# A hybrid two-block transformer kernel: single instructions of ScalarE, VectorE, TensorE and the weight plan put in another order

## The chip, the cores and the metric

The kernel runs on one core of one Trainium2 chip. The metric is the device time in microseconds (us). In the notes below PE is TensorE (matrix products), ACT is ScalarE, DVE is VectorE, POOL is GpSimd and SP is SyncE, whose queue issues the loads of the weights.

## The reference, cut to what matters

256 tokens of width 1024, float32. Two blocks follow each other, of two layers each. In the first block a layer is a mixer of three branches (a chunked state-space scan, "ssd"; a latent attention of four heads, "MLA"; a spatial gate, "gMLP") and a feed-forward stage: dense in layer 0, eight experts with two chosen for each token in layer 1. In the second block the mixer has two attentions (moba, eight heads; diff, four pairs of heads) and the feed-forward stage is dense. Each half of a layer is modulated by a shift, a scale and a gate, which are products of one condition vector with large matrices.

```python
def modulation(c, w, b):
    m = jnp.einsum("bd,de->be", jax.nn.silu(c), w) + b
    shift, scale, gate = jnp.split(m, 3, axis=-1)
...
def hybrid_mixer(h, ...):
    proj = jnp.einsum("btd,de->bte", h, w_in)
    z, xs, bm, cm, dt, q_lat, kv_lat, k_pe, gu, gv = jnp.split(proj, split_at, axis=-1)
    xbc = jax.nn.silu(causal_depthwise_conv(jnp.concatenate([xs, bm, cm], axis=-1), conv_w, conv_b))
    ...
    y_ssd = gated_group_rmsnorm(ssd_scan(xs, bm, cm, dt, a_log, d_skip), z, ssd_norm_w)
    ...
    y = jnp.concatenate([y_ssd, y_mla, y_gm], axis=-1)
    return jnp.einsum("bte,ed->btd", y, w_out)

def swiglu(h, w1, w3, w2):
    a = jnp.einsum("btd,df->btf", h, w1)
    g = jnp.einsum("btd,df->btf", h, w3)
    return jnp.einsum("btf,fd->btd", jax.nn.silu(a) * g, w2)
```

## The kernel before

All weights are read in blocks of 1 MB (128 x 2048 float32), in the order of one list, `plan`, through a ring of six buffers that SP loads. A product keeps float32 accuracy by three matmuls: each operand is split into a rounded high half and the rest, its low half. ACT writes a block's high half (`high_halves`, L1261), DVE its low half in place (`low_halves`, L1956), and PE multiplies (`product`, L497 to L499):

```python
pe.matmul(ps, xh, wh, start=first, stop=False)
pe.matmul(ps, xh, wl, start=False, stop=False)
return pe.matmul(ps, xl, wh, start=False, stop=last)
```

Activations are split in the same way (`hh` and `hl`, `yl`, and `uh`/`ul`, some of which lie in buffers named `PTr`). `ahead` lets the halves run two blocks ahead of the products. Blocks of modulation matrices ("mod") stand in the plan between the others, put there by `weave`; DVE multiplies them with the condition (two instructions each, L1896) when `low_halves` comes to them, before the next low half.

Each engine's program is written out by hand as calls in order (`tensor_program`, `scalar_program`, `vector_program`, `gpsimd_program`, `sync_program`), and an engine does its instructions strictly in that order; semaphores carry the waits between engines. So an instruction that waits holds up whatever stands behind it in its engine's program. The stages follow each other: mixer, feed-forward stage, mixer, experts, mixer, feed-forward, mixer, feed-forward.

The places that the change touches are these. In the first mixer (`mixer1`): on ACT the causal convolution's Silu (`feature_gates`, L1431), behind the taps that DVE sums (L2200); the latents of MLA (L1450); the transposed queries and keys of MLA, which PE leaves in four PSUM banks and which are copied out by `heads_turned`, the second of each pair by ACT (L1469), the first by DVE (L2230), before the scores (L724). On PE, the transposes of the mixer's rows (`to_features`, L579), with eviction by ACT and the low half `yl` by DVE (L2033), and the output blocks 2 and 3, done whole in float32 (`whole_block`, L886), before blocks 0 and 1. On DVE, `gates` (the layer norm of the spatial gate) and `chunk_outputs` (which frees the bank that PE's `within_chunk`, L848, waits for). In `swiglu`: six groups of up to two blocks; `result_block` makes the halves of the block of the second matrix. `layer_rows` (L1990, L1992) applies the previous layer norm's gain and bias to the residual X before a `boundary`. In the second mixer (`mixer2`): twelve projection blocks in the order WIN2, four output blocks; `project` evicts a projection on ACT (L1589) and makes halves ahead; `next(diff)` and `next(moba)` advance the two attentions by a step, DVE evicting turned keys and queries (L2470) and ACT others.

## Time and profile before

| | |
|---|---|
| three runs, us | 2141.05 (median), 2140.62, 2142.23 |
| profiled execution | 2143.6 us |
| its span, first to last instruction | 2141.8 us, 1.8 less |
| mean granted clock of PE | 0.950 |
| busy: PE, DVE, ACT, POOL | 93%, 78%, 55%, 3% |
| DMA, mean over the span | 259 GB/s |

The stages of the span, from and to in us: start 0 to 42, first mixer layer 0 to 191, first ffn 196 to 420, first mixer layer 1 421 to 557, experts to 1394, second mixer layer 0 1410 to 1582, second ffn layer 0 1585 to 1783, second mixer layer 1 1786 to 1946, second ffn layer 1 1948 to 2141.

A profile row gives an instruction's engine, its line, what it writes and reads (`out<-in`), its shape and its time; the releaser of a wait ("<-") is the instruction whose end let the waiting one start. PEclk is the granted clock of PE as a share of full speed.

### The profile page before, as it was taken

To read this page: it belongs to the slowest core of one execution; us is meant where nothing else is said; L and a number is where in the kernel's file an instruction comes from. 1 tells how busy PE (TensorE), PEld (TensorE's weight loads), DVE (VectorE), ACT (ScalarE), POOL (GpSimd) and SP (SyncE) were. 2 spreads that over 40 slices of the span, in tenths; PEclk is the share of its full clock that TensorE was granted. 3 is DMA by queue.
4 is the path that set the end of the run, shared out by engine and by line. 5 is a ranking of instruction groups with operands and counts; after the bars stand their busy time and mean duration, and the time that the engine had idled before them with its cause. 6 is when DMAs were issued, how large, how long until landed. Compare 5 with 4: busy or idle time off the path is not lost.

```text
span 2141.8 us, 28331 instructions
## 1 busy us (share of the span) xinstructions
PE 1985.2 (93%) x11530; PEld 1716.7 (80%) x11530; DVE 1676.3 (78%) x1757; ACT 1169.2 (55%) x1312; POOL 72.7 (3%) x121
## 2 busy tenths in 40 slices
PE   6988999889789999999999999967899999889999
PEld 6776898777578888888788788766789998769998
DVE  6866888776698989899899988888778896855444
ACT  3643334364367767777777767544553445555332
POOL 6001000000100000000000000000010000000000
PEclk8988999898899999999999999988889999989999
DMA  9843899642399999999999999926229995314552
GB/s 352 282 155 138 324 350 352 232 151 93 134 339 328 348 370 354 336 354 374 337 346 358 371 331 354 335 103 229 99 99 352 348 370 169 119 59 141 192 179 99
DMA packets 251209, 554.37 MB, mean 259 GB/s; under 512 B 10076, under 2 KB 75856, under 8 KB 251072
## 3 DMA queue, kind: packets, MB, share of 16 engines
q1 hardware_dynamic: 247252, 544.13, 71.2%
q0 software_dynamic: 3552, 8.29, 1.2%
q8 instruction: 94, 1.54, 0.3%
q14 instruction: 43, 0.35, 0.0%
q10 hardware_dynamic: 268, 0.07, 0.0%
HBM read 551.40 MB, written 1.05 MB: 258 GB/s over the span
## 4 chain that ended last, share of the span: by engine, by line
PE 70%; DVE 14%; ACT 7%; DMA 5%; issue 4%; SPq 0%; ACTq 0%; DVEq 0%
PE bank L497 21%; PE bank L498 20%; PE bank L499 20%; DVE ring_lo L1956 4%; ACT ring_hi L1261 4%; DMA ring<-in_ffn_w_dram 2%; DVE acc L1896 1%; PE bank L886 1%; DMA ring<-in_w_in_dram 1%; DMA ring<-in_ada_w_dram 1%; PE bank L579 1%; PE bank L1086 1%; DVE XN L2200 1%; PE bank L548 1%; DVE work L2138 1%
## 5 line engine op out<-in xcount | busy, mean ns | idle before, releaser
L1956 DVE TENSOR_TENSOR ring_lo<-ring,ring_hi 128x2048 fp32r<-128x2048 f32 x417 | 950.0, 2286 | 270.5 <-ACT ring_hi L1261 267.8
L1261 ACT ACTIVATE ring_hi<-ring 128x2048 fp32r<-128x2048 f32 x417 | 795.5, 1913 | 487.9 <-PE bank L499 237.6
L497 PE MATMUL bank<-hh,ring_hi 128*128 128x256 f32 x1152 | 331.4, 288 | 15.0 <-DVE ring_lo L1956 9.7
L498 PE MATMUL bank<-hl,ring_hi 128*128 128x256 f32 x1152 | 329.2, 286 | 0.0
L499 PE MATMUL bank<-hh,ring_lo 128*128 128x256 f32 x1152 | 328.9, 285 | 0.0
L497 PEld LDWEIGHTS bank<-hh,ring_hi 128*128 128x128 f32 x1152 | 224.2, 195 | 18.9 <-DVE ring_lo L1956 8.6
L499 PE MATMUL bank<-ring_hi,hl 128*128 128x256 f32 (+2 forms) x768 | 238.7, 311 | 0.0
L497 PE MATMUL bank<-ring_hi,hh 128*128 128x256 f32 (+2 forms) x672 | 215.5, 321 | 14.8 <-DVE hl L2020 9.5
L497 PE MATMUL bank<-ring_hi,hgh 128*128 128x512 f32 (+1 forms) x576 | 220.3, 383 | 9.1 <-DVE ring_lo L1956 3.6
L498 PEld LDWEIGHTS bank<-hl,ring_hi 128*128 128x128 f32 x1152 | 224.3, 195 | 0.9 <-issue 0.5
L499 PEld LDWEIGHTS bank<-hh,ring_lo 128*128 128x128 f32 x1152 | 224.4, 195 | 0.0
L499 PE MATMUL bank<-ring_hi,hgl 128*128 128x512 f32 (+1 forms) x576 | 216.3, 376 | 0.0
L498 PE MATMUL bank<-ring_lo,hgh 128*128 128x512 f32 (+1 forms) x576 | 216.2, 375 | 0.0
L498 PE MATMUL bank<-ring_lo,hh 128*128 128x256 f32 (+2 forms) x672 | 209.4, 312 | 0.0
L497 PE MATMUL bank<-ring_hi,uh 128*128 128x512 f32 x496 | 198.7, 401 | 7.0 <-DVE ring_lo L1956 5.9
L498 PE MATMUL bank<-ring_lo,uh 128*128 128x512 f32 x496 | 196.2, 396 | 0.0
L499 PE MATMUL bank<-ring_hi,ul 128*128 128x512 f32 x496 | 196.0, 395 | 0.0
L1896 DVE SCALAR_TENSOR_TENSOR acc<-ring,csil,acc 128x1024 f32<-128x1024 f32 x140 | 179.7, 1283 | 14.2 <-DMA ring<-in_ada_w_dram 7.7
L497 PEld LDWEIGHTS bank<-ring_hi,hh 128*128 128x128 f32 x672 | 136.4, 203 | 30.0 <-issue 17.9
L499 PEld LDWEIGHTS bank<-ring_hi,hl 128*128 128x128 f32 x768 | 151.4, 197 | 6.6
L498 PEld LDWEIGHTS bank<-ring_lo,hh 128*128 128x128 f32 x672 | 136.5, 203 | 5.0 <-issue 0.7
L497 PEld LDWEIGHTS bank<-ring_hi,hgh 128*128 128x128 f32 x576 | 108.2, 188 | 33.9 <-issue 4.9
(426 smaller groups left out, 2795.0 us busy)
## 6 DMA issues: line engine op xcount, KB each, us to landing
ring<-in_moe_w_dram SPq DMA_DIRECT2D x264, 1024.0 KB, 5.3
ring<-in_ada_w_dram SPq DMA_DIRECT2D x48, 1024.0 KB, 8.1
ring<-in_w_mod_dram SPq DMA_DIRECT2D x48, 1024.0 KB, 7.3
ring<-in_w_in_dram SPq DMA_DIRECT2D x40, 1024.0 KB, 6.2
ring<-in_ffn_w_dram SPq DMA_DIRECT2D x33, 1024.0 KB, 6.6
ring<-in_w_gate_dram SPq DMA_DIRECT2D x22, 1024.0 KB, 5.0
ring<-in_w_up_dram SPq DMA_DIRECT2D x22, 1024.0 KB, 5.1
ring<-in_w_down_dram SPq DMA_DIRECT2D x22, 1024.0 KB, 5.1
```

The costliest lines, as they stand in the source:

```text
L497: pe.matmul(ps, xh, wh, start=first, stop=False)
L498: pe.matmul(ps, xh, wl, start=False, stop=False)
L499: return pe.matmul(ps, xl, wh, start=False, stop=last)
L548: x = pe.matmul(ps[:, 8 * j + i:8 * j + i + 1], sums_at(m, j)[0][:, 128 * i:128 * i + 128], ones[:, 0:1], start=True, stop=True)
L579: x = pe.transpose(ban[kk][:, 256 * i + 128 * t:256 * i + 128 * t + 128], src[:, t, 128 * kc:128 * kc + 128], ident)
L886: x = pe.matmul(Y[t][h][:, :], YT[:, 2 * i + k, 128 * t:128 * t + 128], w[:, c:c + 512], start=first and k == 0, stop=False)
L1086: x = pe.transpose(ps[:, 128 * c:128 * c + 128], U[:, 128 * c:128 * c + 128], ident)
L1261: act.activation(ring_hi[i % NH][:, 0:z], ring[n % NS][:, 0:z], ACT.Copy).then_inc(*s.hi(("hi", home(s, i), i)))
L1896: x = dve.scalar_tensor_tensor(v, w[:, k, :], csil[:, col:col + 1], v, ALU.mult, ALU.add)
L1956: dve.tensor_tensor(ring_lo[n % NS][:, 0:z], ring[n % NS][:, 0:z], hi, ALU.subtract).then_inc(*s.lo(("lo", home(s, i), i)))
L2138: dve.tensor_tensor(S, R.of(*A, "scores", i, c)[:, 0:384], mask, ALU.add).then_inc(*vec(("free", *A, "scores", i, c)))
L2200: dve.scalar_tensor_tensor(xv[:, k, :], xc[:, k, j:j + 256], col(j), xv[:, k, :], ALU.mult, ALU.add).then_inc(*vec((*M, "conv", k)))
```

## The change

It moves instructions and takes few away. In order of the program: (1) in the second mixer of layer 0 the eight modulation blocks, woven between the projections before, stand one behind each of blocks 10, 11, 4, 5 and the four output blocks; (2) in the first mixer PE's transposes of the ssd rows stand before whole block 3; (3) in the last group of a dense feed-forward stage the halves of u stand before both result blocks instead of between them; (4) ACT copies all four of the turned queries and keys of MLA; (5) the convolution's Silus of all three blocks stand together behind the latents; (6) in the second mixer the high half of some blocks is made later, the second step of diff attention comes before block 2, on ACT and DVE; (7) the residual's gain and bias rows for the boundary behind the first ffn are done inside and behind that ffn instead of before it; (8) DVE's `gates` comes after `chunk_outputs(0)`.

```diff
@@ -363,7 +363,9 @@
             win2 = [(("win2", l, i), (kview(8, 256), krows(a["w_in_2"][l][:, 256 * i:256 * i + 256]))) for i in WIN2]
-            put_blocks(weave(win2, mods((5, 0), (5, 1)) if l == 0 else []) + rowblocks(("wout2", l), a["w_out_2"][l]))
+            blocks = win2 + rowblocks(("wout2", l), a["w_out_2"][l])
+            for i, b in enumerate(blocks):
+                put_blocks([b] + (mods((5, 0), (5, 1))[i - 8:i - 7] if l == 0 and i >= 8 else []))
             put_blocks(weave(ffn_blocks((("ffn2", l), a["w_gate_2"][l], a["w_up_2"][l], a["w_down_2"][l])),
@@ -929,8 +931,8 @@
                 R2.start()
+                to_features((*M, "yT"), YK, [[(*M, "ssd")]] * 2, range(2))
                 whole_block(3, [], False)
-                to_features((*M, "yT"), YK, [[(*M, "ssd")]] * 2, range(2))
                 last_blocks("wout", l, 0, 1)
@@ -1351,12 +1353,13 @@
                     last = [(groups[G - 1][0], i) for i in results_of(groups[G - 1][1])] if G else []
-                    for x, i in last[:1]:
+                    early = 0 if key[0] != "moe" and g == 5 else 1
+                    for x, i in last[:early]:
                         result_block(s, x, i)
...
                         act.activation(fuh[g % 2][:, 2 * h:2 * h + 2, :], fu[g % 2][:, 2 * h:2 * h + 2, :], ACT.Copy).then_inc(*s.act((s.part, *key, "uh", g, h)))
-                    for x, i in last[1:]:
+                    for x, i in last[early:]:
                         result_block(s, x, i)
@@ -1465,9 +1468,10 @@
                     for nm, dst in (("qT", qTm), ("kT", kTm)):
-                        act.wait_ge(*at(*M, nm, "turned", 1))
-                        act.activation(dst[:, 2:4, :], R.of(*M, nm, 1)[0:96, :].rearrange("p (h c) -> p h c", h=2), ACT.Copy).then_inc(
-                            *main.act((*M, nm, 1), ("free", *M, nm, 1)))
+                        for hp in range(2):
+                            act.wait_ge(*at(*M, nm, "turned", hp))
+                            act.activation(dst[:, 2 * hp:2 * hp + 2, :], R.of(*M, nm, hp)[0:96, :].rearrange("p (h c) -> p h c", h=2), ACT.Copy).then_inc(
+                                *main.act((*M, nm, hp), ("free", *M, nm, hp)))
 
@@ -1536,13 +1540,12 @@
                 feature_block(512)
-                feature_gates(512)
                 feature_block(768)
                 latents_turned()
-                feature_gates(768)
                 feature_block(1024)
                 latents_projected()
-                feature_gates(1024)
+                for c0 in (512, 768, 1024):
+                    feature_gates(c0)
                 decays()
@@ -1580,9 +1583,10 @@
 
-                def project(i, dst, *waits):
+                def project(i, dst, *waits, at_once=False):
                     summed(turn_of["win2", l, i])
-                    high_halves(main, ahead(turn_of["win2", l, i]))
+                    if not at_once:
+                        high_halves(main, ahead(turn_of["win2", l, i]))
                     act.wait_ge(*at(*M, "proj", i))
@@ -1641,16 +1645,16 @@
                 next(diff)
-                halves_for(2)
                 next(diff)
...
                 squares(1)
-                project(10, vt(2))
+                project(10, vt(2), at_once=True)
                 values_in(2)
                 turn_group(0)
+                halves_for(10)
                 next(diff)
@@ -2088,14 +2092,17 @@
                     last = [(groups[G - 1][0], i) for i in results_of(groups[G - 1][1])] if G else []
-                    for x, i in last[:1]:
+                    early = 0 if key[0] != "moe" and g == 5 else 1
+                    for x, i in last[:early]:
                         result_block(s, x, i)
...
                                           fuh[g % 2][:, 2 * h:2 * h + 2, :].bitcast(F32), ALU.subtract).then_inc(*s.vec((s.part, *key, "u", g, h)))
-                    for x, i in last[1:]:
+                    for x, i in last[early:]:
                         result_block(s, x, i)
+                    if key[0] == "ffn" and g == 2:
+                        layer_rows(1, YK, (1,))
                     if key[0] == "moe" and g == 0 and key[1]:
@@ -2224,12 +2231,6 @@
 
-                def heads_turned():
-                    for nm, dst in (("qT", qTm), ("kT", kTm)):
-                        dve.wait_ge(*at(*M, nm, "turned", 0))
-                        dve.tensor_copy(dst[:, 0:2, :], R.of(*M, nm, 0)[0:96, :].rearrange("p (h c) -> p h c", h=2)).then_inc(
-                            *vec((*M, nm, 0), ("free", *M, nm, 0)))
-
                 def time_steps():
@@ -2395,7 +2396,6 @@
                 block("win", 1792)
-                heads_turned()
                 mla = attention((*M, "mla"), mla_heads(l), MLA_SCALE)
@@ -2409,9 +2409,9 @@
                 next(mla)
-                gates()
                 spatial_weights()
                 chunk_outputs(0)
+                gates()
                 block("win", 0)
@@ -2512,11 +2512,11 @@
                 next(diff)
+                next(diff)
                 block("win2", 2)
...
                 block("win2", 3)
-                next(diff)
                 turn_group(0)
@@ -2777,8 +2777,8 @@
             dve.tensor_tensor(rtl[:, :, :], rtr[:, :, :], rth[:, :, :].bitcast(F32), ALU.subtract).then_inc(*vec(("router weights",)))
-            layer_rows(1, YK)
             swiglu(main, ("ffn", 0))
+            layer_rows(1, YK, (0,))
             summed((1, "end"))
```

Three places show the moves. First ACT in the first mixer, layer 1, from the first Silu (L1431 before, L1434 in the changed file) to the evictions of the third feature block (L1416, L1419); XN holds the convolutions, PT the latents. Before:

```order
L1431 ACT_TABLE_LOAD
L1431 ACTIVATE XN<-XN 128x256 x2
L1261 ACTIVATE ring_hi<-ring 128x2048
L1416 ACTIVATE YT<-bank 128x2x256
L1424 ACTIVATE XN<-YT,pA 128x256 x2
L1450 ACTIVATE PT<-bank,pA 128x256 x3
L1431 ACTIVATE XN<-XN 128x256 x2
L1261 ACTIVATE ring_hi<-ring 128x1344
L1416 ACTIVATE YT<-bank 128x2x256
L1424 ACTIVATE XN<-YT,pA 128x256 x2
```

In the changed kernel:

```order
L1263 ACTIVATE ring_hi<-ring 128x2048
L1419 ACTIVATE YT<-bank 128x2x256
L1427 ACTIVATE XN<-YT,pA 128x256 x2
L1453 ACTIVATE PT<-bank,pA 128x256 x3
L1263 ACTIVATE ring_hi<-ring 128x1344
L1419 ACTIVATE YT<-bank 128x2x256
L1427 ACTIVATE XN<-YT,pA 128x256 x2
L1462 ACTIVATE QK<-bank 128x384
...
L1434 ACT_TABLE_LOAD
L1434 ACTIVATE XN<-XN 128x256 x6
```

The table load and the Silus have left the places between the evictions and stand behind the last latents.

Second DVE in the second mixer, layer 0, before its first scores. `acc<-ring` are the modulation gemvs, `ring_lo` the low halves, and the copy QK the evicted turned tile that the scores read. Before:

```order
L2175 TENSOR_TENSOR PT<-XN 128x16x8
L1896 SCALAR_TENSOR_TENSOR acc<-ring2,csil,acc 128x1024 x2
L1956 TENSOR_TENSOR ring_lo3_52<-ring3,ring_hi1 128x2048
L1896 SCALAR_TENSOR_TENSOR acc<-ring4,csil,acc 128x1024 x2
L1956 TENSOR_TENSOR ring_lo5_54<-ring5,ring_hi2 128x2048
L2470 COPY QK<-bank5 128x512
L2440 TENSOR_REDUCE st<-XN 128x16
```

In the changed kernel:

```order
L2181 TENSOR_TENSOR PT<-XN 128x16x8
L2182 TENSOR_TENSOR PT<-XN 128x16x8
L1960 TENSOR_TENSOR ring_lo5_54<-ring5,ring_hi1 128x2048
L1960 TENSOR_TENSOR ring_lo0_49<-ring0,ring_hi2 128x2048
L2470 COPY QK<-bank5 128x512
L2440 TENSOR_REDUCE st<-XN 128x16
```

The gemvs are gone from here; the low halves remain, in other ring slots.

Third ACT at the end of the second ffn, layer 0. `PTr_58<-PT` is the high half of u of the last group, `ring_hi` are high halves of weight blocks, the last two of this stretch those of the second matrix's last block and of the next section's first. Before:

```order
L1261 ACTIVATE ring_hi2<-ring2 128x2048
L1349 ACTIVATE PT<-bank6 128x512
L1261 ACTIVATE ring_hi0<-ring4 128x2048
L1261 ACTIVATE ring_hi1<-ring5 128x2048
L1358 ACTIVATE PTr_58<-PT 128x512
L1261 ACTIVATE ring_hi2<-ring0 128x2048
```

In the changed kernel:

```order
L1263 ACTIVATE ring_hi2<-ring2 128x2048
L1351 ACTIVATE PT<-bank6 128x512
L1263 ACTIVATE ring_hi0<-ring4 128x2048
L1361 ACTIVATE PTr_58<-PT 128x512
L1263 ACTIVATE ring_hi1<-ring5 128x2048
L1263 ACTIVATE ring_hi2<-ring0 128x2048
```

The high half of u has moved in front of the one high half that stood before it.

## Rows read from the trace of the kernel before

**Rows 1.** The page's first part, TensorE: busy us, share of the span, instructions.

```profile
PE 1985.2 (93%) x11530; PEld 1716.7 (80%) x11530; DVE 1676.3 (78%) x1757; ACT 1169.2 (55%) x1312; POOL 72.7 (3%) x121
```

**Rows 2.** What PE waited for, whole span: us in total, times, longest us.

```profile
PE bank L497 <- DVE ring_lo L1956: 21.4, 19, 3.6
...
PE bank L702 <- DVE work L2166: 9.0, 6, 3.5
PE bank L724 <- DVE QK L2470: 8.0, 2, 7.4
PE bank L724 <- DVE QK L2230: 6.3, 2, 5.2
PE bank L497 <- DVE PTr L2095: 6.0, 2, 5.4
...
PE bank L714 <- ACT PT L1589: 5.6, 3, 3.2
...
PE bank L497 <- DVE yl L2033: 4.2, 2, 2.1
PE bank L848 <- DVE YK L2354: 3.7, 2, 2.4
...
PE bank L782 <- ACT YT L1416: 3.1, 1, 3.1
...
PE bank L779 <- ACT PT L1450: 1.9, 1, 1.9
```

**Rows 3.** Windows: us; PE, PEld, DVE, ACT, POOL busy; granted clock; DMA share, GB/s.

```profile
106.70:113.40 6.70, 4.63 (x20) 4.48 (x21) 4.28 (x11) 1.09 (x5) 0.00 (x0) 0.50 0.20 83
174.90:178.30 3.40, 3.40 (x9) 2.69 (x9) 2.28 (x2) 1.30 (x2) 0.00 (x0) 0.50 0.84 328
205.70:209.00 3.30, 3.15 (x14) 3.15 (x15) 3.30 (x3) 0.00 (x0) 0.00 (x0) 0.50 0.20 83
```

**Rows 4.** Timeline of DVE, first mixer, layer 0: start us, us, instruction, [idle <-releaser].

```profile
99.82 5.30 DVE L1896 SCALAR_TENSOR_TENSOR acc<-ring,csil,acc 128x1024 f32<-128x1024 f32 x4
...
107.24 1.28 DVE L2230 COPY QK<-bank 96x512 f32<-96x512 f32 x2
```

**Rows 5.** Timeline of ACT, first mixer, layer 0.

```profile
95.53 1.28 ACT L1500 ACT_TABLE_LOAD   x1
96.83 0.21 ACT L1500 ACTIVATE st<-st 128x8 f32<-128x8 f32 x1
...
103.58 0.59 ACT L1469 ACTIVATE QK<-bank 96x512 f32<-96x512 f32 x1 [0.25 <-PE bank L795]
```

**Rows 6.** Timeline of DVE, start of the first ffn.

```profile
198.72 1.22 DVE L1990 TENSOR_TENSOR X<-XN,YK 128x1024 f32<-128x1024 f32 x1
...
203.51 4.49 DVE L1956 TENSOR_TENSOR ring_lo<-ring,ring_hi 128x2048 fp32r<-128x2048 f32 x2
```

**Rows 7.** Timeline of ACT, end of the first ffn.

```profile
395.10 1.91 ACT L1261 ACTIVATE ring_hi<-ring 128x2048 fp32r<-128x2048 f32 x1 [5.61 <-DMA ring<-in_ffn_w_dram]
```

**Rows 8.** Timeline of ACT, first mixer, layer 1.

```profile
458.89 0.42 ACT L1431 ACTIVATE XN<-XN 128x256 f32<-128x256 f32 x1 [3.30 <-DVE XN L2200]
...
461.86 0.58 ACT L1416 ACTIVATE YT<-bank 128x512 f32<-128x512 f32 x1
```

**Rows 9.** Timeline of DVE, second mixer, layer 0, before the first scores.

```profile
1453.69 2.60 DVE L1896 SCALAR_TENSOR_TENSOR acc<-ring,csil,acc 128x1024 f32<-128x1024 f32 x2
...
1463.12 0.68 DVE L2470 COPY QK<-bank 128x512 f32<-128x512 f32 x1
```

**Rows 10.** Timeline of SP's DMA queue, end of the second mixer, layer 0.

```profile
1565.32 0.37 SPq L2987 DMA_DIRECT2D ring<-in_w_mod_dram  x1
```

**Rows 11.** Timeline of ACT, end of the second ffn, layer 0.

```profile
1763.47 1.92 ACT L1261 ACTIVATE ring_hi<-ring 128x2048 fp32r<-128x2048 f32 x1 [0.60 <-DMA ring<-in_w_down_dram]
1765.83 0.63 ACT L1358 ACTIVATE PTr<-PT 128x512 fp32r<-128x512 f32 x1 [0.44 <-DVE PT L2087]
```

**Rows 12.** The page's DMA issues: count, KB each, median us from issue to landing.

```profile
ring<-in_w_mod_dram SPq DMA_DIRECT2D x48, 1024.0 KB, 7.3
```

## The prediction

> **What bounds the kernel now.** I read the page first: TensorE (PE) is busy 1985.2 us, 93% of the span [rows 1], so the time is PE's work plus its idle time, and every part of the change aims at idle time. Next the waits of PE, summed by what ended them [rows 2]: single waits stand there (7.4, 5.2, 5.4, 3.6, 3.5, 3.2 and 3.1 us), nearly all ended by VectorE (DVE) or ScalarE (ACT). Then, for each wait, the timeline of the engine that ended it, to see what stood in front of the awaited instruction. Last the clock: three short stretches behind such waits where PE ran at 0.50 of full speed, the lower of its two levels, 1.2 GHz [rows 3]. Ahead of each the engine had stood idle, and a wait that goes may take the stretch with it. PE was busy there 4.63, 3.40 and 3.15 us at half speed, so 2.3, 1.7 and 1.6 us are the most that each can give back.
>
> The sum is made against the profiled execution, 2143.6 us (span 2141.8 and 1.8 around it). It lies 2.55 above the median of the runs, 2141.05.
>
> **First mixer, layer 0.** *Heads.* The first MLA scores waited 5.2 us for DVE's copies of the first halves of qT and kT (the longest of line 724's two, [rows 2]). DVE had four modulation gemvs from 99.82 on, then a low half, and ended the copies at 108.52 (107.24 plus 1.28, [rows 4]). ACT had its own two copies done at 104.17 [rows 5]. With all four on ACT, two copies of 0.59 come on top, back to back, less an overlap of 0.1: about 105.2. PE starts about 3.4 us earlier; I add 0.3 of clock and take -3.7. If ACT's line is later by one high half (1.9) it is -1.8; if the whole half-clock stretch goes, 2.3 [rows 3], it is -5.7.
>
> *Convolutions together.* The six Silus move behind the latents, with one table load before and one after as before. In layer 0 PE and DVE are busy until 101, so I price this at nothing, hidden behind the gate differences that DVE makes meanwhile; without that cover it would cost the table load. The row says that a table load costs 1.28 us and that the next activation starts 0.02 later [rows 5]. The Trainium skill (ScalarE: Activation LUTs, What ACT_TABLE_LOAD costs) puts a switch at about 2.7 us including a drain; by it the moved load in front of the exponentials would make ACT some 1.4 us later, this term -2.4 instead of -3.7, and the sum 1.3 smaller. This trace does not agree: no such drain stands behind the load.
>
> *ssd transposed before the last whole block.* In both layers PE waited for the low half of the ssd rows, 4.2 us in 2 waits [rows 2]. The sixteen matmuls of whole block 3 now lie between the transposes and their use and cover the eviction chain. -2.1 in each; in layer 0 the half-clock stretch behind it (174.9 to 178.3, [rows 3]) may give 1.7, of which I take 0.9: -3.0. Bounds 0 and -3.8.
>
> *gates() later.* It held the release of a bank for within_chunk(1): 3.7 us in 2 waits, the longer 2.4 [rows 2]. In layer 0 I take the whole shorter one, 1.3, with a little clock, -1.7; in layer 1 another DVE result is due directly behind, so half of the 2.4, -1.15. Bounds 0 and -3.7 for both.
>
> Layer 0: -3.7 -3.0 -1.7 = **-8.4**.
>
> **First ffn.** The four operations on the residual's scale and shift rows, 1.22 us each, filled DVE from 198.72 to the first low half at 203.51 [rows 6]; PE waited 3.6 for that low half (longest of its 19, [rows 2]) and then ran at half clock (205.7 to 209, [rows 3]). Both go: -3.6 -1.6 = -5.2. The four are not gone: the two for tile 1 come behind group 2, between low halves (0 to 0.9, taken 0.4); the two for tile 0 stand before the boundary's first residual, 2.4 us of which DVE's idle time there hides most: +0.8. In the last group the half of w2's block 10 waited for its DMA, 5.61 us [rows 7], so putting the halves of u in front saves at most 0.7 of the 5.4 wait and I take 0.2. Net **-4.0** (-4.6 to -1.5).
>
> **First mixer, layer 1.** The Silus waited for DVE's convolutions (3.30 before the one at 458.89) with the evictions of latents and of xc behind them in ACT's queue [rows 8]: PE waits of 1.9 and 3.1 [rows 2]. Both go, 5.0; then DVE's own chain (convolutions, rotations, differences) is next and keeps half. -2.5 (0 to -5). With -1.15 and -2.1 from above: **-5.7**.
>
> **Second mixer, layer 0.** Eight modulation blocks (sixteen gemvs, eight pairs of 2.60) move from between the projections to behind blocks 10, 11, 4, 5 and the four output blocks. Before the first scores DVE did two pairs and two low halves, 9.4 us from 1453.69 to the copy at 1463.12 [rows 9], and PE waited 7.4. Without them that wait goes. ACT's change of order takes the 3.2 (longest of line 714's three on PT) and about 3.5 of line 702's waits [rows 2]. That is -14.1. Given back: the eight pairs, 20.8 us, now fall where PE waits for DVE's softmax. Of them I let 6.6 reach PE, an estimate: 2.7 at the fourth scores, where a pair and a low half (2.6 and 2.3) now stand in front of the copy, half of which PE covers with the matmuls of a block; 1.4 in moba's normalizations; 2.5 at the output blocks. At the end, the first gate block's load waited for nothing before; now it takes the slot of the next to last output block, freed where the row at 1565.32 stands [rows 10], and takes its landing and its two halves from there; its low half lands among the boundary's residuals, +2.8. Sum -14.1 +6.6 +2.8 = **-4.7**, with no clock counted. Bounds: -10 if 1.3 of the pairs reach PE, +4 if three quarters of them do (15.3).
>
> **Second ffn, layer 0.** Here the reordering costs. The high half of block 10 started at 1763.47 and the half of u, which waits for DVE, at 1765.83 [rows 11]. In the new order the high half stands behind the wait: it starts at 1766.4 instead, 2.9 later, its low half follows, and PE, which stood 0.6 then, stands about 2.6. With a little clock **+2.2** (+1.5 to +3.2). In layer 1's ffn the same order costs nothing; there the load comes early and PE's work on the blocks before covers the wait.
>
> **Second mixer, layer 1.** No modulations. The 3.5 at line 702 and 2.2 on PT [rows 2] go by the order of ACT and DVE; DVE takes back some 1.7. **-4.0** (-1.5 to -6).
>
> **The sum**: -8.4 -4.0 -5.7 -4.7 +2.2 -4.0 = -24.6, and I take 0.6 off for halves rounded my way: -24. 2143.6 - 24 = 2119.6; less the 2.55 to the median: **2117 us**. The MoE stage between is untouched and shifts as a whole.
>
> **Rivals.** *DVE takes back what PE gains.* Each wait that goes leaves DVE next, and DVE's order is rigid. Then the second mixer's layer 0 comes to 0 and the rest gives half: -8.4/2 -4.0 -5.7/2 +2.2 -2.0, about -11: **2130**. For it: all long waits but four were ended by DVE [rows 2]. Against it: in the first mixer's layer 0 and the first ffn the DVE work itself is removed or moved to where PE has its input.
> *More clock.* All three stretches of [rows 3] and others like them go: 5 to 8 us more, **2110**. For it: each follows a wait that goes. Against: new short waits arise nearby.
> *Slower: DVE stands for modulation blocks.* Such a block took 7.3 us from issue to landing [rows 12], and in the new plan its load comes right behind its neighbour's, in a ring whose slots the second mixer frees slowly. If DVE, which works in order, stood for each of the eight, softmax and low halves behind it would stand too. From 28.3/8 = 3.5 us for each block the whole kernel is more than 0.2% slower; at 4 us, +32 on 2117: **2149**. Against it: six slots give a lead of several blocks.
> *Nothing moves:* that the waits merely shift to the next instruction everywhere, within 4.3 us of 2141, is hard to reconcile with the first ffn and the first heads, -7.7 between them.
>
> **How the numbers follow.** The forecast with its bounds (2110 to 2125) 0.58; DVE takes back (2125 to 2136) 0.22; more clock (below 2110) 0.08; nothing moves 0.07; slower 0.05. The range that holds 8 in 10 is 2109 to 2133. A measurement tells about 0.2%, 4.3 us, from no change: faster 0.87, same 0.07, slower 0.06.
>
> **What would show it.** In the changed kernel: line 724's first wait in layer 0 near 1.5 us, released by ACT; no wait on the ssd low half; the first low half of the first ffn right behind the halves of its input, with full clock; the first diff scores without a wait over 1 us, and a new one of 2 to 3 at the fourth; the wait for the half of u near 2.6 at the end of the second ffn's layer 0. Wrong it would be if DVE showed waits on modulation DMAs of over 1 us each, if the second mixer's layer 0 took as long as before, or if the half-clock stretches stayed behind shorter waits.

## The result and the profile after

The changed kernel takes 2116.9 us (median of four runs, 2111.56 to 2117.56) against 2140.84 before (four runs): a ratio of 0.9884, 95% interval 0.9865 to 0.9903, 23.9 us faster. The prediction was 2117.

That the total was met does not mean that its terms were. The table compares the stages of the profiled executions. A stage is taken from the first product on its input to the first product of the next one, and each number is the stage's length less its length before (us). "Again" is the changed kernel in a second set of runs.

| | start | mixer 1, l. 0 | ffn 1 | mixer 1, l. 1 | experts | mixer 2, l. 0 | ffn 2, l. 0 | mixer 2, l. 1 | ffn 2, l. 1 | span |
|---|---|---|---|---|---|---|---|---|---|---|
| before, length | 42.4 | 153.9 | 225.0 | 140.2 | 855.4 | 168.9 | 201.0 | 161.9 | 193.2 | 2141.8 |
| predicted | 0 | -8.4 | -4.0 | -5.7 | 0 | -4.7 | +2.2 | -4.0 | 0 | |
| changed | -0.3 | -11.8 | -9.0 | -5.4 | +0.7 | -3.5 | +3.7 | -6.3 | 0.0 | 2109.7 |
| again | -0.4 | -11.5 | -8.6 | -3.8 | -1.1 | -3.7 | +3.3 | -6.3 | -1.4 | 2108.3 |

The profiled execution is the shortest of its four, 5.3 us below their median, while the one of before lay 2.55 above its own. So the two profiles differ by 32.1 us of span, 8 more than the medians. A half-clock stretch that lies across the end of a stage moves about a microsecond between two columns: 1.1 us of the +3.7 of the second ffn's layer 0, and of the -6.3 behind it, is one such stretch.

The page's first part and PE's waits in the changed kernel, in the columns of [rows 1] and [rows 2] (lines have moved down by up to seven):

```profile
PE 1974.4 (94%) x11530; PEld 1709.2 (81%) x11530; DVE 1672.8 (79%) x1753; ACT 1171.0 (56%) x1316; POOL 72.6 (3%) x121
```

```profile
PE bank L499 <- DVE ring_lo L1960: 23.3, 19, 3.1
...
PE bank L581 <- DVE YK L2335: 10.4, 2, 6.9
...
PE bank L726 <- DVE QK L2470: 4.9, 4, 3.2
PE bank L797 <- ACT PT L1412: 4.4, 1, 4.4
...
PE bank L704 <- DVE work L2173: 2.6, 2, 1.4
...
PE bank L716 <- ACT PT L1593: 2.2, 1, 2.2
...
PE bank L726 <- ACT QK L1473: 2.0, 2, 1.1
```

Against [rows 2], the waits on the ssd low half (4.2), at within_chunk (3.7) and on latents and xc (1.9 and 3.1) are gone, the scores' 5.2 is 1.1, and the 7.4 before the first diff scores is gone. Two waits are as large as those that went and were not forecast: 10.4 us in two before the transposes of the gMLP rows (L581, was 2.5), and 4.4 at the turning of MLA's queries (L797, was 0.3). Their rows before were:

```profile
PE bank L579 <- DVE YK L2334: 2.5, 2, 1.3
...
PE bank L795 <- ACT PT L1409: 0.3, 1, 0.3
```

PE's busy time also fell by 10.8 us with the same 11530 matmuls, so many of them ran faster. Two windows of the changed kernel that answer to [rows 3], in the columns used there:

```profile
100.00:107.00 7.00, 5.93 (x50) 5.66 (x50) 6.83 (x5) 4.56 (x7) 0.00 (x0) 1.00 0.55 200
188.00:195.00 7.00, 7.00 (x61) 7.00 (x60) 6.86 (x5) 4.64 (x3) 0.00 (x0) 1.00 0.37 108
```

The heads' scores and the start of the first ffn now run at full clock, where before PE ran at half after its waits of 5.2 and 3.6 us. Not every such stretch went: 176.8 to 187.1 us is at 0.50, across the end of layer 0 (188.6 to 195.4 before), and 449.9 to 456.7, from within the new wait of 4.4 on, is new.

### The profile page after: what moved, and what is told of

Its sections match the earlier page's. It is cut to its first block, busy times and chain, and to the rows that moved or that the text cites. A ratio compares the mean times of both kernels' runs of the same rounds, so it can differ in the third digit from the quotient of the medians.

```text
span 2109.7 us, 28332 instructions
## 1 busy us (share of the span) xinstructions
PE 1974.4 (94%) x11530; PEld 1709.2 (81%) x11530; DVE 1672.8 (79%) x1753; ACT 1171.0 (56%) x1316; POOL 72.6 (3%) x121
## 4 chain that ended last, share of the span: by engine, by line
PE 74%; DVE 13%; ACT 6%; DMA 3%; issue 3%; SPq 0%; ACTq 0%; DVEq 0%
PE bank L499 22%; PE bank L500 22%; PE bank L501 21%; DVE ring_lo L1960 4%; ACT ring_hi L1263 3%; DVE acc L1900 2%; PE bank L888 1%; DMA ring<-in_w_in_dram 1%; PE bank L581 1%; DMA ring<-in_ffn_w_dram 1%; PE bank L550 1%; PE bank L1088 1%; DMA ring<-in_ada_w_dram 1%; DVE work L2145 1%; DVE XN L2207 1%
## 5 line engine op out<-in xcount | busy, mean ns | idle before, releaser
L499 PE MATMUL bank<-ring_hi,hh 128*128 128x256 f32 (+2 forms) x672 | 214.5, 319 | 10.4 <-DVE hl L2024 9.4
```

## The experiments

Twelve kernels ran: the changed one again, four that undo one part each, and seven that build on what was seen. Parts 2, 4, 6 and 7 were not undone by themselves, so what they are worth is read from the traces of before and after alone. "Changed" below is the changed kernel.

**The changed kernel again.** No edit.

> The changed kernel unaltered, as the yardstick of the runs beside it and for a second trace: its four runs so far are 2111.6 once and 2116.3 to 2117.6 three times, and the one that was profiled is the short one. If the 5 us lie in one stage (a half-clock stretch there or not, or the end of the first ffn, whose loads run at 0.96 of the DMA), this trace has that stage longer and the others within 0.5 us; if the runs merely scatter, the difference is spread over several stages. Median expected 2112 to 2118.

Median 2115.3 us (2110.15 to 2119.71), ratio 0.9887 (0.9869 to 0.9906). The trace was again of a short execution (2110.15), so it could not show where a long one spends its 5 us. It agrees with the first within 0.5 us in six stages; layer 1 of mixer 1, the experts and the last ffn differ by 1.4 to 1.9. Other runs helped: the first ffn, whose code is the same in all of them, was -3.6 in the run with the modulations back and -9.0 in changed. The window of the same 20 us in the two (columns of [rows 3], the last two the DMA), changed first:

```profile
360.00:380.00 20.00, 16.86 (x107) 14.97 (x106) 17.46 (x13) 9.41 (x7) 0.00 (x0) 0.96 1.01 363
```

```profile
360.00:380.00 20.00, 18.80 (x127) 17.01 (x126) 17.05 (x14) 6.86 (x5) 0.00 (x0) 1.00 0.91 330
```

It moved 363 GB/s in the one and 330 in the other, and a block of that ffn took 5.3 and 7.2 us to land (6.6 before). The last wait of the ffn was 3.1 in the one and 5.1 in the other. Several microseconds of this stage therefore belong to the execution, not to the kernel. That the long runs are those with slow loads fits, but was not shown.

**Part 8 undone**: `gates()` in front of `chunk_outputs(0)` again.

```diff
+                gates()
                 spatial_weights()
                 chunk_outputs(0)
-                gates()
                 block("win", 0)
```

> Undoes part 8 alone: DVE's gates() stands before chunk_outputs(0) again, in both layers of the first mixer. Theory one, that this part saved the two waits of 1.36 and 2.35 us at L848 as the prediction has it: slower by 2 to 4 us than the changed kernel. Theory two, that DVE's whole chain up to the gMLP rows (L2335) sets the end of this place: the waits at the within_chunk matmuls come back (about 1.4 and 2.4 us) and the waits of 3.5 and 6.9 us before the transposes (L581) get shorter by as much, and the time stays within 1 us, except for what the clock does, up to 4 us slower if the half-clock stretch at 509 to 526 of the kernel before returns.

Median 2118.94 us (2113.42 to 2121.3), ratio 0.9906 (0.9890 to 0.9923), which overlaps with changed. The two waits among PE's waits of this run, in the columns of [rows 2]:

```profile
PE bank L581 <- DVE YK L2335: 4.4, 2, 3.1
...
PE bank L850 <- DVE YK L2355: 3.5, 2, 2.5
```

Together 7.9, where changed has 10.4 and 0, and PE ran more slowly between the two: against the changed kernel again, PE was level in the span ahead of layer 1's first wait, 2.6 us later behind it, 6.8 before the second, and 1.3 behind it. The second wait takes up most of what was won or lost ahead of it. In this the waits follow theory two: DVE's chain sets the end of this place. The time does not: PE stayed 1.3 us later behind it in layer 1 and 0.8 in layer 0, and the median is 3.6 above that of the changed kernel beside it, with overlapping intervals, which is nearer to theory one. What DVE's chain is stands in the timeline of DVE in changed, layer 1 (columns of [rows 4]):

```profile
485.36 2.60 DVE L1900 SCALAR_TENSOR_TENSOR acc<-ring,csil,acc 128x1024 f32<-128x1024 f32 x2
487.87 4.48 DVE L1960 TENSOR_TENSOR ring_lo<-ring,ring_hi 128x2048 fp32r<-128x2048 f32 x2
...
495.10 1.12 DVE L2335 SCALAR_TENSOR_TENSOR YK<-bank,pA,PT 128x128 f32<-128x128 f32 x4
```

A pair of gemvs and two low halves, 7 us, stand in front of the rows that PE waits for. The low halves belong to output blocks 0 and 1, which PE reaches only behind two whole blocks.

**Part 3 undone**: `early = 1` in both `swiglu`.

> Undoes part 3 alone: the halves of u of the last group stand between the two result blocks again. Theory one (prediction's term of +2.2 for the second ffn of layer 0, and -0.2 to -0.7 for the first ffn): the wait of 2.5 us for the last block's low half in the second ffn falls to about 0.6, that stage is 2 to 3.5 us shorter, the first ffn 0.7 longer; in all 1.5 to 3 us faster than the changed kernel. Theory two, that the 2.3 us which the first ffn's last wait lost (5.45 to 3.14) came from this part: the first ffn 2.3 longer, the second 3 shorter, together within 1 us.

Median 2111.91 us (2108.19 to 2117.83), ratio 0.9879 (0.9859 to 0.9898). The second ffn's layer 0 is 2.7 to 3.0 us shorter than in the two profiles of changed, and its last wait falls from 2.5 to 1.0: theory one for this stage. The first ffn is 1.0 to 1.5 longer, less than its scatter, so what this part is worth there stays undecided (the second mixer's layer 0, whose code is the same, was 2.5 shorter). The median is 3.4 below that of the changed kernel beside it, with overlapping intervals.

**Part 1 undone**: the modulation blocks woven between the projections again.

```diff
-            blocks = win2 + rowblocks(("wout2", l), a["w_out_2"][l])
-            for i, b in enumerate(blocks):
-                put_blocks([b] + (mods((5, 0), (5, 1))[i - 8:i - 7] if l == 0 and i >= 8 else []))
+            put_blocks(weave(win2, mods((5, 0), (5, 1)) if l == 0 else []) + rowblocks(("wout2", l), a["w_out_2"][l]))
```

> Undoes part 1 alone: the eight modulation blocks are woven between the projections again, the rest of the second mixer's new order stays. Theory one, that the moved gemvs gave that stage's gain: the wait of about 7 us before the first diff scores returns, the new one of 3.2 us at the fourth scores goes, as do the late low half at the boundary (about 2.8 us), and the stage is 0.5 to 4 us longer than in the changed kernel. Rival, that ACT's and DVE's new order alone gave it and the moved gemvs cost as much as they save: the stage 0 to 4 us shorter than in the changed kernel. The other stages within 0.5 us.

Median 2121.35 us (2117.97 to 2128.57), ratio 0.9924 (0.9904 to 0.9944). The second mixer's layer 0 is 3.8 to 4.0 longer than in changed, and together with the ffn behind it 1.6 to 2.2 longer: theory one for the stage's length. PE's waits of this run at the diff scores:

```profile
PE bank L724 <- DVE QK L2468: 11.8, 4, 7.4
```

The 7.4 is back. The 3.2 at the fourth scores is there too, but that does not clear the gemvs: woven in, a pair of them stands in front of that copy as well. DVE ahead of the copy, in changed and then in this run (columns of [rows 4]):

```profile
1452.32 2.60 DVE L1900 SCALAR_TENSOR_TENSOR acc<-ring,csil,acc 128x1024 f32<-128x1024 f32 x2
1454.83 2.29 DVE L1960 TENSOR_TENSOR ring_lo<-ring,ring_hi 128x2048 fp32r<-128x2048 f32 x1
1457.03 0.69 DVE L2470 COPY QK<-bank 128x512 f32<-128x512 f32 x1
```

```profile
1467.74 2.60 DVE L1898 SCALAR_TENSOR_TENSOR acc<-ring,csil,acc 128x1024 f32<-128x1024 f32 x2
1470.26 2.28 DVE L1958 TENSOR_TENSOR ring_lo<-ring,ring_hi 128x2048 fp32r<-128x2048 f32 x1
1472.46 0.68 DVE L2468 COPY QK<-bank 128x512 f32<-128x512 f32 x1
```

The waits of 1.6 and 1.2 us at the boundary are gone but for one of 0.5.

**Part 5 undone**: `feature_gates` between the evictions again.

> Undoes part 5 alone: the convolutions' Silus stand between the evictions again. In the changed kernel the waits of 1.9 and 3.1 us on the latents and xc of layer 1 are gone, but a wait of 4.35 us at the turning of the queries (L797) on ACT's eviction of projection 1792 is new. Theory one: that wait is the Silus' price (ACT comes to the eviction late because it stands for DVE's convolutions in front of it). Then it goes here, 1.9 and 3.1 return, and layer 1 of the first mixer is 0.3 to 2 us longer than in the changed kernel. Rival, the prediction's term: DVE's chain behind the convolutions sets both, and that layer is 2 to 3.5 us longer. Layer 0 within 0.5 us by both.

Median 2118.65 us (2114.1 to 2124.98), ratio 0.9905 (0.9885 to 0.9925). In layer 1 the waits of 1.9 and 3.1 returned and the one at L797 fell from 4.4 to 1.1. The layer is -4.8 against -5.4 and -3.8 in the two profiles of changed: no difference, the low end of theory one. Layer 0 was 3.2 to 3.5 us longer than in changed, which neither theory expected: waits of 0.5 and 0.8 on ACT came up at L784 and L797, and the rest is spread.

**Low halves later.** In `mixer1` on DVE, `block("win", 0)` and `block("win", 256)` move from in front of the second chunk to behind `spatial()`.

> One change on top of the changed kernel: in the first mixer DVE makes the low halves of output blocks 0 and 1 (and the gemvs before them) behind the gMLP rows instead of in front of the second chunk's outputs. Theory (from the run with gates() back): the waits of 3.5 and 6.9 us before the transposes (L581) are DVE's chain behind these two low halves, 4.5 us in layer 0 and 7.1 with the gemvs in layer 1, which PE needs only some 17 us later, after two whole blocks. Then both waits fall below 1 us and the two layers are 3 and 5 to 6.5 us shorter. Rival: the chain is bound by what DVE waits for from PE and ACT (the last attention values, the states), or the low halves come late for output block 0: the waits only shrink by 1 to 2 us or come back at L499, and the gain is below 2 us in all.

Median 2117.41 us (2114.3 to 2125.22), ratio 0.9902 (0.9882 to 0.9922): no gain; layer 0 was 2.2 to 2.6 us longer than in changed and layer 1 no shorter. PE's waits of this run:

```profile
PE bank L888 <- issue: 9.2, 2, 6.1
...
PE bank L581 <- DVE YK L2335: 2.5, 2, 1.3
```

The wait at L581 fell as the theory had it, and came back at whole block 2 (L888). The low halves now stood in front of DVE's copy of the turned rows, `late_features`. The idea held and the place was wrong.

**Eviction first.** On ACT, layer 1 only: `token_block(1792, 256)` in front of `differences(0)`, with `block(1792)` behind `heads_turned()`.

> One change on top of the changed kernel: in layer 1 of the first mixer ACT evicts projection 1792 right behind the decays, in front of the gates' differences and of the next high half, which is made behind the four turned heads. Theory: the new wait of 4.35 us (L797) is this eviction standing behind the differences (which wait for DVE) and a high half of 1.9; it falls below 1 us and the layer is 2.5 to 4.5 us shorter. Rival: the high half made 2 to 3 us later delays its low half and the next product, and DVE's differences bound the scores anyway: gain below 1.5 us.

Median 2111.2 us (2105.11 to 2116.96), ratio 0.9866 (0.9843 to 0.9889). The wait at L797 is gone and one of 3.65 us at the scores (L726, on ACT's copies) took its place: the copies stood behind the differences, which wait for DVE. The layer is as long as in changed.

**All three**: these two, and part 3 in the first ffn only.

> The two changes above together, and the halves of u of the last group in the old place in the second block's feed-forward stages only. If the three are independent: 3 + 6 + 3 + 2.8 = about 14 us faster than the changed kernel, near 2102; if the gains in the first mixer are eaten by the loads of the first ffn and of the experts (0.9 to 1.0 of the DMA), only 3 to 8, near 2108 to 2112.

Median 2112.22 us (2105.71 to 2112.47), ratio 0.9860 (0.9840 to 0.9880). The second ffn's layer 0 is +0.6 instead of +3.7; the rest is as in the two runs above, with 10.5 us waited at L888.

**The three, placed anew.** The low halves behind the ssd rows, and the heads in front of the differences:

```diff
                 spatial()
                 late_features()
                 outputs()
+                block("win", 0)
+                block("win", 256)
...
+                    token_block(1792, 256)
+                    heads_turned()
+                    differences(0)
+                    block(1792)
```

> The three changes again, two of them placed by what the last runs showed. The low halves of output blocks 0 and 1 now stand behind the ssd rows: in the run before they stood in front of DVE's copy of the turned gMLP rows, and the wait that left the transposes (L581) came back as 4.0 and 6.5 us in front of whole block 2 (L888). The turned heads of layer 1 are evicted right behind projection 1792, in front of the gates' differences: in the run before the wait only moved, 3.65 us at the scores. Theory: the waits at L581 and L888 are then both below 1.5 us in both layers and the one at the scores below 1.5; first mixer 2.5 to 4 us shorter in layer 0 and 6 to 9 in layer 1 than in the changed kernel, the whole at 2101 to 2106. Rival: the next link holds the same end, the ssd rows (ACT's squares and table load) or the late low halves at the products of output block 0 (L499): then less than half of it, 2107 to 2112.

Median 2104.52 us (2100.93 to 2111.56), ratio 0.9840 (0.9820 to 0.9860), the first that is clearly faster than changed. Layer 0 is 3.6 to 4.0 shorter, and the waits at L581 and L888 are 1.3 and 0.7. Layer 1 gained nothing (-5.8), although its scores came 7.0 us earlier in the span than in changed (5.1 counted from the layer's first product). One wait and the clock behind it gave that back. In this run, PE's wait, then DVE's timeline ahead of it (columns of [rows 4]), then two windows behind it (columns of [rows 3]):

```profile
PE bank L832 <- DVE gate L2326: 4.6, 2, 3.6
```

```profile
448.99 2.29 DVE L1966 TENSOR_TENSOR ring_lo<-ring,ring_hi 128x2048 fp32r<-128x2048 f32 x1 [2.63 <-ACT ring_hi L1263]
```

```profile
454.00:464.00 10.00, 9.90 (x48) 9.51 (x47) 3.88 (x10) 3.03 (x9) 0.00 (x0) 0.50 0.01 2
464.00:474.00 10.00, 10.00 (x44) 7.71 (x44) 4.70 (x11) 3.54 (x12) 0.00 (x0) 0.50 0.28 105
```

DVE stood 2.63 us for ACT's high half with the softmax and the differences queued behind it, PE waited 3.6, and then ran 20 us at half clock. In changed the clock was back at full by 457:

```profile
452.00:460.00 8.00, 7.07 (x44) 6.49 (x43) 5.68 (x17) 3.36 (x9) 0.00 (x0) 0.70 0.00 0
460.00:470.00 10.00, 10.00 (x86) 8.83 (x85) 4.74 (x11) 4.85 (x16) 0.00 (x0) 1.00 0.32 107
```

**Modulations one block earlier**, on top of that: `[i - 7:i - 6]` and `i >= 7` in place of `[i - 8:i - 7]` and `i >= 8`.

> As the run beside it, with the eight modulation blocks one block earlier in the plan (behind block 3 first, the last output block has none behind it). Theory: the late first gate block was a cost of the eighth modulation behind the last block; the waits of 1.6 and 1.2 us at the boundary of the second mixer's layer 0 fall below 0.5 each, no gemv comes in front of the first scores, and the second mixer of layer 0 with the ffn behind it is 1.5 to 3 us shorter than beside it. Rival: the pair of gemvs that comes earlier costs the same in front of the fourth scores or in the softmax: within 1 us.

Median 2103.5 us (2101.83 to 2111.06), ratio 0.9837 (0.9818 to 0.9856). The two waits at the boundary are gone but for one of 0.5, and the second mixer's layer 0 with its ffn is 3.5 shorter than beside it (-6.7 against -3.2), a little over the theory's 1.5 to 3. The medians differ by 1 us, within their scatter.

**The low half behind the softmax**, on top of that, in layer 1 on DVE:

```diff
-                block("win", 1792)
+                if l == 0:
+                    block("win", 1792)
                 mla = attention((*M, "mla"), mla_heads(l), MLA_SCALE)
                 next(mla)
                 differences(1)
+                if l == 1:
+                    block("win", 1792)
```

> On top of the run with the modulations one block earlier: in layer 1 of the first mixer DVE makes the low half that belongs to projection 1792 behind the first softmax step and the second chunk's gate differences, not in front. In the last two runs the scores came 7 us earlier than in the changed kernel, but DVE stood 2.63 us for the high half with softmax and differences behind it, PE waited 3.63 us at L832, and then ran at half clock from about 454 to 474, which gave all of it back. Theory: with the low half behind, that wait falls below 1.5 us; if the half-clock stretch goes with it, the layer is 6 to 10 us shorter than beside it and the whole at 2094 to 2099; if the stretch stays, only 2 to 3, at 2100 to 2102. Rival: the low half comes late for its product, a wait of 2 us or more at L499 takes the place, within 1.5 us.

Median 2091.56 us (2086.52 to 2095.41), ratio 0.9773 (0.9749 to 0.9796): faster than the changed kernel by 24 us, about as much as that was faster than before. Layer 1 is -17.2, 10.3 shorter than in the run before. PE's waits of this run at L832, and the same two windows:

```profile
PE bank L832 <- DVE gate L2326: 1.0, 1, 1.0
```

```profile
454.00:464.00 10.00, 9.76 (x86) 8.96 (x84) 8.32 (x19) 5.51 (x16) 0.00 (x0) 1.00 0.09 13
464.00:474.00 10.00, 10.00 (x84) 9.28 (x83) 7.86 (x13) 6.94 (x14) 0.00 (x0) 1.00 0.34 105
```

The one wait left at L832 is layer 0's; layer 1 has none, and PE did 170 matmuls in these 20 us instead of 92. It is not one lucky execution: layer 1 was -5.8 and -6.9 in the two runs without this edit and -17.2 and -17.9 in the two with it (the next run has the same layer 1), and the medians of this run and of the one before are 12 us apart, with intervals that do not meet.

**The same in both layers**: in layer 0, too, `block("win", 1792)` stands behind `differences(1)`.

> As the run beside it, in both layers. In layer 0 four gemvs (5.3 us) stand in front of that low half; with softmax and differences ahead of them the wait at L832 (1.0 us) goes and the scores' chain starts earlier. Theory: layer 0 is 1 to 3 us shorter than beside it. Rival: the gemvs then hold up the next step of DVE or their slots come free later and loads with them: layer 0 the same or up to 3 us longer.

Median 2097.64 us (2092.69 to 2103.15), ratio 0.9813 (0.9791 to 0.9834). The wait at L832 in layer 0 goes and one of 3.6 us at L815, on ACT, takes its place. Layer 0 is -10.3, 1.8 shorter than beside it, but the same code as beside it was -13.5 one run earlier, so this decides nothing. The medians speak against it, 6 us longer with intervals that touch, while the two profiles are alike (spans of 2090.9 and 2091.1). Where a typical execution loses the time was not seen.

## Why the prediction was right, and where it was not

The direction, the total and most mechanisms held. That the median fell on 2117 itself is in part luck: single terms missed by up to 5 us, and the profiled executions gained 8 more than was priced. The rival that DVE would stand for modulation blocks did not come: in the second mixer's layer 0 DVE waited for no DMA in the trace of changed. By the prediction's steps:

- **Heads**: -3.7 was too small by about 1. The scores start 4.1 us earlier in the span and the whole half-clock stretch went, 2.2 more, a little past the far bound of -5.7. But two new waits of 1.0 and 0.4 on DVE's gate differences (L832, L835) follow and took 1.7 back, so that PE's lead over the kernel before was 4.5 us behind them. The scores' wait is 1.1, released by ACT, as forecast.
- **Convolutions together**: both waits went, as forecast. Of the lead that this gave PE, 3.0 us was left at the scores and 1.8 behind the new half-clock stretch there, where 2.5 was forecast. The rest went to a wait of 4.4 on ACT's own queue (eviction of projection 1792 behind the differences, which wait for DVE, and a high half). It was this order and not DVE's chain that held the scores: placed anew, they came 5.1 us earlier with DVE's work ahead of them unchanged. Undone, layer 1 was the same. In layer 0 this part was put at nothing, hidden behind the gate differences; undone, that layer was 3.2 to 3.5 longer, so some of its -11.8 belongs here. In front of the exponentials the trace shows no drain behind the table load either: in changed it starts at 443.89, takes 1.28, and the next activation starts at 445.18.
- **ssd before the whole block**: -3.0 in layer 0 was too small. PE's lead grew by 2.4 from ahead of the moved transposes to behind the old wait and by 1.6 in the old half-clock stretch, in all just past the far bound of -3.8. In layer 1 it grew by 2.4 (2.1 forecast).
- **gates() later**: priced at -1.7 and -1.15. The waits of 1.4 and 2.4 at within_chunk went, but they were not the last on that path: the wait for the gMLP rows right behind grew from 1.3 to 3.5 in layer 0 and from 1.3 to 6.9 in layer 1, because these rows stand behind two low halves on DVE. Clock included, PE's lead grew by 3.1 and 1.5 across this place; undoing the part cost 0.8 and 1.3 there. So the size of the step held within 1.5 us, but the path did not: the prediction has no term for the low halves.
- **First ffn**: -4.0 against -9.0 and -8.6. The first wait and its half-clock went as priced (3.8 and 1.5), a half-clock stretch that now lies over the stage's first products took 1.3, and one new wait of 1.4 came up 30 us later. The term that was mis-sized is the end of the stage: the last wait fell from 5.4 to 3.1 where at most 0.7 was allowed, and shorter waits on the way went too, though the change moves no load of this stage. The same code gave -3.6 to -9.0 in other executions.
- **Second mixer, layer 0**: -4.7 against -3.5 and -3.7. The wait before the first scores went, and the fourth scores wait 3.2 (2.7 forecast) behind a pair of gemvs and a low half, as forecast. The late first gate block cost 1.6 and 1.2 at the boundary (2.8 forecast), and moving the blocks up by one removed all but 0.5 of it.
- **Second ffn, layer 0**: +2.2 against +3.7 and +3.3, with a wait of 2.5 (2.6 forecast). The run that undid it gave 2.7 to 3.0 back. The term that spoke against the change was right, and its part is a loss.
- **Second mixer, layer 1**: -4.0 against -6.3, just past the far bound (-6), or about -5.2 without the stretch that lies across its start. The wait of 3.5 went whole and the half-clock stretch behind it with it; the one of 2.2 on PT stayed, against the forecast; DVE took back less than priced.

The terms sum to -24.6, the two traces to -32.1 and -33.5, and the medians to -23.9 and -24.7. The profiled executions gained more than priced, chiefly in the first mixer's layer 0 and the first ffn. Much of the excess is clock. In the first trace PE's idle time fell by 21.3 us and its busy time by 10.8; in the second, from the line below, by 17.9 and 15.6. The prediction has some 3 us of clock among its terms and the rest in waits.

```profile
PE 1969.6 (93%) x11530; PEld 1704.4 (81%) x11530; DVE 1672.9 (79%) x1753; ACT 1171.0 (56%) x1316; POOL 72.5 (3%) x121
```

The prediction counted three half-clock stretches, and the trace of before holds more: the one of 144.2 to 157.9, behind a wait of 1.4 at within_chunk, is 146.1 to 149.5 in the changed kernel. So the rival of more clock is what the profiled executions came to, 2111.56 and 2110.15; the medians did not. Typical executions lie about 5 us above those profiled, and by their number the total was met. What separates the two is not settled.

Three sums of the working are off by 0.1 to 0.3 and move nothing: the first ffn's terms give -4.2 and not -4.0, three quarters of the pairs are 15.6 and not 15.3, and 1.4 us on the heads' term gives -2.3 and not -2.4.

## What to carry to other kernels

Before pricing a removed wait in full, follow the awaited engine's queue to the next instruction that PE will need: here three of the freed waits came back within 20 us, in whole or in large part, on the same engine. A half that is made ahead belongs behind what is needed sooner: here the place of one low half in the queue, not its duration, was worth 10 us. And when an edit gains nothing, look for the one new wait behind it before dropping the edit: the run that gave nothing in layer 1 was one moved line from giving 10 us.

## What the runs showed of the hardware

A wait cost far more in clock than in itself: 3.6 us at L832 was followed by 20 us at half clock, which alone is worth 10 by an estimate from PE's busy time in them, half of 19.9. But the same code does not always meet it alike. In the run with the modulations one block earlier the same wait was followed by 13.7 us at half clock:

```profile
459.20:472.90 13.70, 13.70 (x67) 12.82 (x66) 4.04 (x10) 3.73 (x13) 0.00 (x0) 0.50 0.20 71
```

A shorter wait shows it more plainly. In layer 0 the wait at L832 was 1.0 us in this run and in the one after it, whose code is the same there; the granted clock behind it was 0.50 in the run with the low half behind the softmax in layer 1 and 1.00 in the other. The two windows, in this order (columns of [rows 3]):

```profile
112.40:122.60 10.20, 10.20 (x48) 9.78 (x47) 2.12 (x4) 3.06 (x9) 0.00 (x0) 0.50 0.05 7
```

```profile
112.00:122.00 10.00, 10.00 (x85) 8.83 (x85) 4.91 (x10) 4.79 (x16) 0.00 (x0) 1.00 0.46 148
```

So that layer was 8.5 us shorter than before in the first and 13.5 in the second. Single profiles of this kernel cannot tell edits apart by a stage's length alone when they are worth less than about 5 us; the place of a wait can be read from one, its price only from several runs.
